# Local attention with folded score blocks: 128 scores and one turn per head, masks made on three engines

## The reference

```python
# per block n of 128 queries: keys of block n-1 and of block n, 256 in all
scores = einsum('bnqhgd,bnshd->bnhgqs', qb, kk) * 64 ** -0.5
dist = qi + BLOCK - kj                      # qi 0..127, kj 0..255
valid = (dist >= 0) & (dist < WINDOW) & (key_pos >= 0)      # WINDOW = 128
scores = where(valid, scores - slope * dist, -inf)
m = maximum(max(scores), sink)
p = exp(scores - m); p = p / (sum(p) + exp(sink - m))
o = einsum('bnhgqs,bnshd->bnqhgd', p, vv)
```

## Time and profile before

| | us |
|---|---|
| median of 3 executions | 2218.82 (2215.28 to 2219.25) |
| the profiled execution | 2216.79, its span 2215.1 |
| TensorE (PE) busy | 2163.8, 98% of the span |
| VectorE (DVE) busy | 1424.1, 64% |
| ScalarE (ACT) busy | 1001.4, 45% |
| GpSimd (POOL) busy | 446.3, 20% |

### The profile page before, as it was taken

How to read it: one execution, slowest core, us unless ns; L and a number is a source line. 1 busy time by engine, 2 the same in 40 slices (tenths; PEclk the granted TensorE clock), 3 DMA queues, 4 the chain that set the end, 5 groups by cost and what they waited for, 6 DMA issues and landing times.

```text
span 2215.1 us, 29323 instructions
## 1 busy us (share of the span) xinstructions
PE 2163.8 (98%) x10792; PEld 1789.0 (81%) x10792; DVE 1424.1 (64%) x2142; ACT 1001.4 (45%) x1809; POOL 446.3 (20%) x344
## 2 busy tenths in 40 slices
PE   7999999999999999999999999999999999999997
PEld 6887888888778887878888887888888888887886
DVE  5776578556866786857567675568655656554555
ACT  5554455545554555543433333346533333333444
POOL 1231023102220222133233330000322222210000
PEclk9999999999999999999999999999999999999999
DMA  4231432353234323643446565888432323227766
GB/s 124 86 124 58 132 96 77 100 162 100 60 111 153 115 67 110 214 138 107 143 140 229 209 233 188 261 270 259 160 121 96 119 91 120 94 93 237 224 210 215
DMA packets 261534, 323.86 MB, mean 146 GB/s; under 512 B 16400, under 2 KB 167952, under 8 KB 261392
## 3 DMA queue, kind: packets, MB, share of 16 engines
q1 hardware_dynamic: 261392, 321.98, 44.3%
HBM read 244.85 MB, written 77.07 MB: 145 GB/s over the span
## 4 chain that ended last, share of the span: by engine, by line
PE 89%; DVE 5%; ACT 2%; issue 2%; DMA 1%; SPq 0%; DVEq 0%; ACTq 0%
PE M L1193 10%; PE M L1195 10%; PE M L1194 9%; PE M L895 7%; PE M L897 6%; PE M L896 6%; PE M L1219 3%; PE M L1220 3%; PE M L1221 3%; PE X L1219 3%; PE X L1220 3%; PE X L1221 3%; PE X L1195 3%; PE X L1193 3%; PE X L1194 3%
## 5 line engine op out<-in xcount | busy, mean ns | idle before, releaser
L2161 DVE TENSOR_TENSOR ring_lo<-ring_raw,ring_hi 128x1024 fp32r<-128x1024 f32 x154 | 188.6, 1225 | 170.6 <-ACT ring_hi L1606 170.4
L895 PE MATMUL M<-uhi,whi 128*128 128x512 f32 (+1 forms) x720 | 285.6, 397 | 3.7 <-DVE wlo L1703 2.1
L1703 DVE TENSOR_TENSOR wlo<-raw,whi 128x1024 fp32r<-128x1024 f32 x120 | 157.9, 1316 | 202.8 <-ACT whi L1254 202.4
L897 PE MATMUL M<-uhi,wlo 128*128 128x512 f32 (+1 forms) x720 | 278.7, 387 | 0.0
L896 PE MATMUL M<-ulo,whi 128*128 128x512 f32 (+1 forms) x720 | 278.3, 386 | 0.0
L1606 ACT ACTIVATE ring_hi<-ring_raw 128x1024 fp32r<-128x1024 f32 x154 | 163.3, 1061 | 233.6 <-DMA ring_raw<-a_scr 230.4
L1193 PE MATMUL M<-t_hi,wu_hi 128*128 128x512 f32 x616 | 240.9, 391 | 3.5 <-DVE gq L2079 2.6
L1195 PE MATMUL M<-t_hi,wu_lo 128*128 128x512 f32 x616 | 240.4, 390 | 0.0
L1194 PE MATMUL M<-t_lo,wu_hi 128*128 128x512 f32 x616 | 240.1, 390 | 0.0
L1254 ACT ACTIVATE whi<-raw 128x1024 fp32r<-128x1024 f32 x120 | 126.7, 1056 | 202.8 <-PE M L897 120.3
L2047 DVE TENSOR_TENSOR wu_lo<-fraw,wu_hi 128x512 fp32r<-128x512 f32 x132 | 124.4, 951 | 123.0 <-ACT wu_hi L1546 122.7
(11 more groups left out here) (275 smaller groups left out, 4967.2 us busy)
## 6 DMA issues: line engine op xcount, KB each, us to landing
raw<-in_w_in_dram SPq DMA_DIRECT2D x88, 512.0 KB, 3.9
ring_raw<-a_scr SPq DMA_DIRECT2D x154, 256.0 KB, 3.5
fraw<-in_w_gate_dram SPq DMA_DIRECT2D x44, 512.0 KB, 4.1
fraw<-in_w_up_dram SPq DMA_DIRECT2D x44, 512.0 KB, 4.9
a_scr<-au SPq DMA_DIRECT2D x88, 256.0 KB, 2.4
ring_raw<-t_scr SPq DMA_DIRECT2D x88, 256.0 KB, 3.0
ring_raw<-in_w_down_dram SPq DMA_DIRECT2D x66, 256.0 KB, 3.0
raw<-in_w_out_dram SPq DMA_DIRECT2D x32, 512.0 KB, 3.9
```

Source lines behind the costliest of these rows:

```text
L895: mm(bank, whi[s][:, kb, :], hi, start=first, stop=False)
L897: return mm(bank, wlo[s][:, kb, :], hi, start=False, stop=last)
L1703: V.tensor_tensor(wlo[s][:, :, :], raw[s][:, :, :], whi[s][:, :, :].bitcast(F32), ALU.subtract).then_inc(s_lo[s], 1)
L2161: V.tensor_tensor(lo[:, :, :], raw_r[:, :, :], hi[:, :, :].bitcast(F32), ALU.subtract).then_inc(s_rowlo, 1)
```

## The change

The 256 scores of a head are folded into 128: for column k of query q, the score of the previous block is put over that of the own block where k > q. One set of 128 is then biased, reduced, exponentiated, normalised and turned. After the turn, the part of the own block is cut out by a bit mask, and the part of the previous block is what is left when it is subtracted.

- TensorE: `p_turn` does 2 transposes a step where it did 4, and waits for one semaphore more, `s_pcur` of the step before. `pv` still does 4 products and waits for `s_pprev` where it waited for `s_pT`.
- VectorE: `scores` begins with a `copy_predicated` of 2x128 in the bank X[0]; its other row operations shrink from 2x256 to 2x128. New is `p_current` in slot i+4, behind `scores`: a bitwise and of X[1] with a mask into the second half of `pT`.
- ScalarE: exponentials of 128 where they were 256, and the copy of X[1] is 256 where it was 512.
- GpSimd: `normalise` is 256 wide where it was 512; the copy of `dist` is gone; new is `p_previous` in slot i+4, behind `key_steps`: a subtraction, 256 wide. A few more masks are made at the start.
- In the first block of all (it = 0, b = 0), whose previous block does not exist, the masked entries come from `dist0`.

```diff
@@ block.tensor: p_turn, pv
                 if i:
                     pe.wait_ge(s_pT, it * STEPS + i)
+                    pe.wait_ge(s_pcur, it * STEPS + i)
                 else:
                     pe.wait_ge(s_vals, it + 1)
-                for n in range(4):
+                for n in range(2):
                     last = tr(X[1][:, n * P:(n + 1) * P], pr[i % 2][:, n * P:(n + 1) * P], ident[:, :])
...
-                pe.wait_ge(s_pT, it * STEPS + i + 1)
+                pe.wait_ge(s_pprev, it * STEPS + i + 1)
...
-                                  pT[i % 2][:, (2 * par + kb) * P:(2 * par + kb + 1) * P],
+                                  pT[i % 2][:, (2 * kb + par) * P:(2 * kb + par + 1) * P],
@@ block.scalar: scores, p_turn
-                    half = pr[w][:, par * 256:(par + 1) * 256]
+                    half = pr[w][:, par * BLOCK:(par + 1) * BLOCK]
...
-                A(pT[i % 2][:, :], X[1][:, :], ACT.Copy).then_inc(s_pT, 1)
+                A(pT[i % 2][:, 0:2 * P], X[1][:, 0:2 * P], ACT.Copy).then_inc(s_pT, 1)
@@ block.vector: scores, p_current, slots
-                d = dist0 if b == 0 else dist
+                d = dist0 if it == 0 and b == 0 else dist
+                both = X[0][:, :].rearrange("p (h k) -> p h k", h=2)
+                V.copy_predicated(both[:, :, 0:BLOCK],
+                                  upto_row[:, :].bitcast(I32).rearrange("p (o k) -> p o k", o=1)
+                                  .broadcast_to([P, 2, BLOCK]), both[:, :, BLOCK:2 * BLOCK]).then_inc(s_fold, 1)
+                dve.wait_ge(s_fold, it * STEPS + i + 1)
                 for par in range(2):
...
-                    last = V.scalar_tensor_tensor(out=pr[w][:, half], in0=d[:, :], scalar=8.0 * slope,
-                                                  in1=X[0][:, half], op0=ALU.mult, op1=ALU.add)
+                    last = V.scalar_tensor_tensor(out=pr[w][:, par * BLOCK:(par + 1) * BLOCK], in0=d[:, :],
+                                                  scalar=8.0 * slope, in1=both[:, par, 0:BLOCK],
+                                                  op0=ALU.mult, op1=ALU.add)
...
-                V.tensor_reduce(mx[:, :], pr[w][:, :].rearrange("p (h k) -> p h k", h=2), AX_X,
+                V.tensor_reduce(mx[:, :], pr[w][:, 0:2 * BLOCK].rearrange("p (h k) -> p h k", h=2), AX_X,
...
+            def p_current(it, i):
+                dve.wait_ge(s_pT, it * STEPS + i + 1)
+                if i >= 2:
+                    dve.wait_ge(s_pv, it * STEPS + i - 1)
+                V.tensor_tensor(pT[i % 2][:, 2 * P:4 * P].rearrange("p (h q) -> p h q", h=2).bitcast(I32),
+                                X[1][:, 0:2 * P].rearrange("p (h q) -> p h q", h=2).bitcast(I32),
+                                upto_column[:, :].bitcast(I32).rearrange("p (o q) -> p o q", o=1)
+                                .broadcast_to([P, 2, P]), ALU.bitwise_and).then_inc(s_pcur, 1)
...
+                    i = step_at(slot, P_TURN)
+                    if i is not None:
+                        p_current(it, i)
@@ block.gpsimd: normalise, p_previous, slots
-                pool.wait_ge(s_rd, it * STEPS + i + 1)
-                halves = pr[i % 2][:, :].rearrange("p (h k) -> p h k", h=2)
+                pool.wait_ge(s_den, 2 * (it * STEPS + i) + 2)
+                halves = pr[i % 2][:, 0:2 * BLOCK].rearrange("p (h k) -> p h k", h=2)
                 G.tensor_tensor(halves, halves, rd[:, :].rearrange("p (h o) -> p h o", o=1)
-                                .broadcast_to([P, 2, 2 * BLOCK]), ALU.mult).then_inc(s_prob, 1)
-                if i == (PAIRS - 1) * TB + 1:
-
-                    pool.wait_ge(s_bias, it * STEPS + i)
-                    copy(dist0[:, :], dist[:, :]).then_inc(s_dist, 1)
+                                .broadcast_to([P, 2, BLOCK]), ALU.mult).then_inc(s_prob, 1)
+
+            def p_previous(it, i):
+
+                pool.wait_ge(s_pT, it * STEPS + i + 1)
+                pool.wait_ge(s_pcur, it * STEPS + i + 1)
+                turned, current = pT[i % 2][:, 0:2 * P], pT[i % 2][:, 2 * P:4 * P]
+                G.tensor_tensor(turned, turned, current, ALU.subtract).then_inc(s_pprev, 1)
...
                         if a is not None:
                             step(it, a)
+                    i = step_at(slot, P_TURN)
+                    if i is not None:
+                        p_previous(it, i)
```

More of the change, by code:

```diff
@@ L226, in block_program @@
         gu = [at(f"gu{i}", (P, T), gu_at + 2 * K * i) for i in range(2)]
-        dist = at("dist", (P, 2 * BLOCK), dist_at)
-        dist0 = at("dist0", (P, 2 * BLOCK), dist_at + K)
+        dist = at("dist", (P, BLOCK), dist_at)
+        dist0 = at("dist0", (P, BLOCK), dist_at + 512)
+        upto_row = at("upto_row", (P, BLOCK), dist_at + K)
+        upto_column = at("upto_column", (P, BLOCK), dist_at + K + 512)
         causal = at("causal", (P, P), dist_at + 2 * K)
@@ L419, in block_program @@
         s_mx = sem("s_mx")
-        s_nm = sem("s_nm")
+        s_fold = sem("s_fold")
         s_nms = sem("s_nms")
@@ L423, in block_program @@
         s_den = sem("s_den")
-        s_rd = sem("s_rd")
+        s_pcur = sem("s_pcur")
         s_prob = sem("s_prob")
@@ L1695, in parameters @@
                 V.tensor_scalar(nsinks[:, :], sinks[:, :], -1.0, None, ALU.mult).then_inc(s_ini2, 1)
-                V.tensor_copy(causal[:, :].bitcast(I32), causal[:, :]).then_inc(s_ini2, 1)
-                dve.wait_ge(s_ini2, 11)
+                for mask in (causal, upto_column):
+                    V.tensor_copy(mask[:, :].bitcast(I32), mask[:, :]).then_inc(s_ini2, 1)
+                dve.wait_ge(s_ini2, 12)
             def make_lo(it, n):
@@ L2256, in _ @@
             G.memset(causal[:, :], -1.0).then_inc(s_ini, 1)
-            G.iota(dist[:, :].bitcast(I32), [[1, 2 * BLOCK]], base=-BLOCK, channel_multiplier=-1).then_inc(s_ini, 1)
+            G.iota(dist0[:, :].bitcast(I32), [[1, BLOCK]], base=0, channel_multiplier=-1).then_inc(s_ini, 1)
             pool.wait_ge(s_ini, 6)
@@ L2262, in _ @@
                             pattern=[[1, P]], channel_multiplier=-1).then_inc(s_ini, 1)
-            G.tensor_copy(dist0[:, :], dist[:, :].bitcast(I32)).then_inc(s_ini, 1)
+            G.tensor_copy(dist[:, :], dist0[:, :].bitcast(I32)).then_inc(s_ini, 1)
             pool.wait_ge(s_ini, 8)
             G.memset(causal[0:CHUNK, CHUNK:P], 0.0).then_inc(s_ini, 1)
-            G.affine_select(out=dist0[:, :], in_=dist0[:, :], compare_op=ALU.is_ge, fill=MASKED, base=BLOCK,
-                            pattern=[[-1, 2 * BLOCK]], channel_multiplier=1).then_inc(s_dst, 1)
@@ L2270, in _ @@
-            pool.wait_ge(s_dst, 1)
-            G.affine_select(out=dist[:, :], in_=dist0[:, :], compare_op=ALU.is_ge, fill=MASKED, base=-1,
-                            pattern=[[1, 2 * BLOCK]], channel_multiplier=-1).then_inc(s_dst, 1)
+            G.iota(upto_row[:, :].bitcast(I32), [[1, BLOCK]], base=-BLOCK, channel_multiplier=-1).then_inc(s_ini, 1)
+            pool.wait_ge(s_ini, 10)
+            G.affine_select(out=dist0[:, :], in_=dist[:, :], compare_op=ALU.is_ge, fill=0.0, base=0,
+                            pattern=[[-1, BLOCK]], channel_multiplier=1).then_inc(s_dst, 1)
@@ L2273, in _ @@
+            G.tensor_copy(upto_column[:, :], upto_row[:, :].bitcast(I32)).then_inc(s_dst, 1)
             pool.wait_ge(s_dst, 2)
-            G.tensor_copy(dist0[:, BLOCK:2 * BLOCK], dist[:, BLOCK:2 * BLOCK]).then_inc(s_dst, 1)
-            G.memset(dist0[:, 0:BLOCK], MASKED).then_inc(s_dst, 1)
+            G.affine_select(out=upto_column[:, :], in_=upto_column[:, :], compare_op=ALU.is_ge, fill=0.0, base=-1,
+                            pattern=[[1, BLOCK]], channel_multiplier=-1).then_inc(s_dst, 1)
@@ L2276, in _ @@
+            pool.wait_ge(s_dst, 3)
+            G.tensor_tensor(dist[:, :], dist0[:, :], upto_column[:, :], ALU.add).then_inc(s_dst, 1)
             pool.wait_ge(s_dst, 4)
-            pool.wait_ge(s_ini, 9)
+            for mask in (upto_row, upto_column):
+                G.memset(mask[:, :], -1.0).then_inc(s_dst, 1)
+            G.affine_select(out=dist0[:, :], in_=dist[:, :], compare_op=ALU.is_ge, fill=MASKED, base=0,
+                            pattern=[[-1, BLOCK]], channel_multiplier=1).then_inc(s_dst, 1)
@@ L2279, in copy @@
+            pool.wait_ge(s_dst, 7)
+            G.affine_select(out=upto_row[:, :], in_=upto_row[:, :], compare_op=ALU.is_ge, fill=0.0, base=0,
+                            pattern=[[-1, BLOCK]], channel_multiplier=1).then_inc(s_dst, 1)
+            G.affine_select(out=upto_column[:, :], in_=upto_column[:, :], compare_op=ALU.is_ge, fill=0.0, base=0,
+                            pattern=[[1, BLOCK]], channel_multiplier=-1).then_inc(s_dst, 1)
+            pool.wait_ge(s_dst, 9)
             def copy(out, in_):
```

19 lines of the change are left out of this document (8 added, 11 removed).

## The result

| | us |
|---|---|
| before, median of 4 runs | 2218.04 (2215.28 to 2219.25) |
| after, median of 4 runs | 2254.84 (2254.14 to 2256.78) |
| ratio | 1.0167, 95% interval 1.0155 to 1.0179 |
| the profiled execution of after: span | 2253.5 (before 2215.1) |

Slower by 36.8 us, 1.7%. The forecast was 2255, its range 2229 to 2271.

What follows compares the result with a forecast made beforehand. TensorE, busy 98% of the span, was taken as the bound. Transposes -13.7, `head_turn` +3.9, `pv` +36.4 and clock +12 make +38.6 us on 2216.8: 2255 us, range 2229 to 2271.

Steps and rivals of the forecast that it cites:

- Transposes, -13.7: TensorE at `p_turn`: 128 transposes fewer, at 0.107 us each, gain 13.7 us.
- VectorE's lateness, 0.28: VectorE's queue: fold and mask outweigh shorter bias and reduction, so all behind `scores` comes 0.28 us later, bounds 0.1 and 0.55.
- `head_turn`, +3.9: TensorE waits longer for VectorE's `sqo` at `head_turn`: 8 places, 0.49 us each, cost 3.9 us.
- `pv`, +36.4: TensorE at `pv` waits for GpSimd's subtraction queued behind `kstate`: 12 places, mean 3.03 us, cost 36.4 us.
- Clock, +12: TensorE's clock falls to half speed behind 7 of the 12 new waits, 1.7 us each: +12 us, between 0 and 20.
- The feed-forward part, the same to a microsecond: Sign to look for in the changed kernel's profile: the feed-forward part keeps its time to a microsecond.
- full speed throughout: Rival: the waits at `pv` come as worked out, but TensorE's clock never falls; 2243 us, chance 0.24.
- No turn-taking: Rival: VectorE's `wlo` and GpSimd's subtraction run beside each other and the clock holds; 2229 us, chance 0.07.
- the lower bound at `pv`: Least cost of TensorE's waits at `pv`, if `wlo` never delays the subtraction: 1.9 us a place, +22.6 us.
- Faster: Rival: the subtraction reaches `pv` in time, so only the turns and `head_turn` count; 2207 us, chance 0.08.

## Why the prediction was right

The mechanism, its places and nearly all its prices are as put. That 2255 was met to 0.2 us is luck all the same: `pv` was priced 3.8 us too high, `head_turn`, `st` and the wait in the down projection together 3.6 too low. Point by point:

- **Transposes, -13.7.** Right as far as can be told: 12.8 by the kernel with two turns, give or take 1.5.
- **VectorE's lateness, 0.28.** Right for the chain: from the first of the score operations to `cuminv` it was 295.43 - 293.66 = 1.77 us, and after it 302.45 - 300.40 = 2.05. The fold takes 0.42 (I had 0.41), the mask 0.42 with 0.34 from start to start. What I missed is that slot 6 has a turn to lose as well: its `wlo` takes 1.55 where it took 1.22.
- **`head_turn`, +3.9.** It was +5.2. Slot 11 waits 1.38 (0.83 before, my +0.49 a little low), slot 16 1.40 to 1.66, slot 21 as before. I also held that all else stays: `st` waits 4 times more, +1.5.
- **`pv`, +36.4.** The mechanism and the places are as put: slots 7, 12, 17 and no others. Slot 7: 3.04 forecast, 3.07 measured; slot 12: 2.79 and 2.90 to 3.09. Within slot 7 two errors cancel. `kstate` was 1.34 us late where I had 1.10, the rest took 1.72 where I had 1.94. Slot 17 is the term that was off: I took 3.27 between 3.84 and 2.69 and it measured 1.92 to 2.16. Half of that is that the subtraction always slips in ahead of `wlo` there. The other half is that `kstate` is less late: 1.41 us in stretch 1 (it ends at 400.72, and `pv` is due at 399.31), where I had 1.90. TensorE comes later itself, by the 0.3 us that `head_turn` in slot 16 waits beyond my +0.49; the rest is open.
- **Clock, +12.** 11.9 measured, 7 falls at 1.7 us each. But behind `pv` 6 of 12 places fell, not 7; the seventh is the fall at 1407 us, told below, in a part where I had expected no change. My 7 of 12 was a guess at half, so the match is luck in part.
- **The feed-forward part, the same to a microsecond.** Wrong by my own measure: from its first matmul to the end it is 1286.8 us before and 1289.8 after. But the change is not shown to be the cause. Of the 13 profiles, the six with no fall of the clock between 1100 us and the last 20 us have 1285.0 to 1287.9, the kernel without the fold among them, with 12 waits on `pT`. The seven with one or two falls there have 1288.3 to 1291.2, the kernel before with two transposes among them, with no such wait. All 11 of these falls stand behind a wait of TensorE in the down projection (on `ring_lo`) of 1.8 to 2.6 us; the 15 waits there without a fall took 0.9 to 2.1. In the profile after it is this one:

```profile
1405.00:1410.00 5.00, 3.46 (x10) 2.76 (x11) 2.45 (x2) 1.92 (x3) 0.00 (x0) 0.75 0.90 326
1410.00:1415.00 5.00, 5.00 (x21) 4.10 (x21) 2.45 (x2) 1.56 (x3) 0.00 (x0) 0.91 0.53 165
```

The rival "full speed throughout" would have been 2243. It falls by the windows: waits of 2 to 3 us brought the clock down. The Trainium skill (TensorE: Matmul & The Clock Gate, "Why this matters for your kernels") names only long idle gaps as the cause. The waits that I forecast, of 2.8 to 3.3 us, were already about as long as it means, so the rule spoke less clearly for this rival than the prediction has it; by it waits of about 2 us should have been harmless. Here gaps of 1.4 to 2.2 us, between short products, were followed by the half clock 12 times in 31. "No turn-taking" falls by the kernel with `wlo` moved. Its price was wrong besides: slot 17 held only half of the 1.15 us, so the rival was 2243 - 8 x 1.15 - 4 x 0.58 = 2231 and not 2229, and the lower bound at `pv` +24.9 and not +22.6. "Faster", at 2207, is what the same change gives with the subtraction first, 2212: my point from which it decides, the end of `kstate` against the start of `pv`, was the right one to look at.

## What to carry to other kernels

When work is hung onto an engine that is 20% busy, ask not how much room it has but what stands in its queue at that instant, and what that waits for. Compare, in the trace, the end of the instruction ahead with the start of the one that will wait; here 0.4 us late already meant 3 us a time, and the idle gap that would have held the work lay right ahead of it. Then price what a wait brings along: the clock, and turns lost between GpSimd and VectorE. And an order moved to win one wait must be followed to the end of the queue, where it may be paid back.

## What was not expected of the hardware

- A fall of the clock cost the same 1.7 us in nearly every case; three were twice as long (at 75 and 198 us in the kernel with the subtraction first for head 1, at 820 us in the one without the fold). Waits at `pv` of 2.4 to 3.1 us were followed by one in 20 of 24 places, waits there up to 1.2 us in none of 13. But at `head_turn` 1.25 us was enough in slot 21 in 9 of 38 places, while 1.38 to 1.83 us in slots 11 and 16 did it once in 60.
- A fall can hide in a wait: TensorE, slower, came to `pv` later and waited 0.62 us where it waits 2.14. So not each 1.7 us reaches the end.
- Which of GpSimd and VectorE asks first is decided by 0.07 to 0.20 us (292.51 against 292.61, 400.68 against 400.75, 295.21 against 295.01), and the loser's instruction is recorded with the wait inside: 0.74 us of subtraction as 1.71, 1.22 of `wlo` as 1.93. The mean of such a group in a profile (0.90 us for the subtraction) is not its price.
